# Second block of a two-block layer stack: projections with the weight tile stationary, so that they land transposed, and the forget bias added by VectorE

## What is computed

```python
h = x @ w_in                       # 2048 x (8*1536 + 12 + 4096)
qa, ka, va, za, qb, kb, vb, zb, f_logit, g_logit = split(h)
out_a = dilated_mixture(rope(qa), rope(ka), va)      # 12 heads of 128
log_f = log_sigmoid(f_logit + b_forget)              # 12 heads
out_b = softmax(qb kb^T * scale + D_t - D_s, causal) @ vb   # D = cumsum(log_f)
up_a = (out_a * silu(za)) @ w_up_a ; up_b = (out_b * silu(zb)) @ w_up_b
g_a, g_b = split(sigmoid(g_logit + b_gate))
y = (g_a * up_a + g_b * up_b) @ w_out
x = layer_norm(ALPHA * x + y, ln_g, ln_b)
```

## Time and profile before

| | |
|---|---|
| device time, median of 3 executions | 3028.01 us (3026.76 to 3030.45) |
| span of the profiled execution, first to last instruction | 3023.4 us |
| the profiled execution's own device time | not given apart from its span; the median is 4.6 us above the span |
| TensorE matmul busy | 2865.6 us (95%), 13536 matmuls |
| TensorE weight loads busy | 2356.3 us (78%) |
| VectorE busy | 1837.2 us (61%) |
| ScalarE busy | 1352.6 us (45%) |
| mean granted TensorE clock | 0.986 of 2.4 GHz |

### The profile page before, as it was taken

One profiled execution on the slowest core, in us unless ns is written; L12 is line 12 of the kernel. 1 busy time (PEld: TensorE's weight loads), 2 busy tenths in 40 slices (PEclk: granted clock), 3 DMA queues, 4 the chain that ended last, 5 costly groups with the idle time before them and its releaser, 6 DMA issues.

```text
span 3023.4 us, 38084 instructions
## 1 busy us (share of the span) xinstructions
PE 2865.6 (95%) x13536; PEld 2356.3 (78%) x13536; DVE 1837.2 (61%) x2035; ACT 1352.6 (45%) x1741; POOL 76.7 (3%) x88
## 2 busy tenths in 40 slices
PE   1699999899998999999999999979999999999997
PEld 1578887688887888888888888858888888788886
DVE  8888988677854655555444455565555544444565
ACT  1244554445543444444444444434445444444442
POOL 0400000000000000000000000010000000000000
PEclk9899999999999999999999999989999999999999
DMA  9887679576544555566554465635554654555663
GB/s 369 282 301 268 236 259 323 205 242 217 168 153 158 188 176 173 173 186 197 168 180 155 166 189 188 216 128 174 180 176 160 207 191 158 166 175 163 195 212 133
DMA packets 165005, 601.15 MB, mean 199 GB/s; under 512 B 19120, under 2 KB 19264, under 8 KB 163808
## 3 DMA queue, kind: packets, MB, share of 16 engines
q1 hardware_dynamic: 160336, 583.08, 57.3%
q0 software_dynamic: 4496, 15.74, 1.8%
HBM read 596.64 MB, written 2.10 MB: 198 GB/s over the span
## 4 chain that ended last, share of the span: by engine, by line
PE 66%; DVE 1%; issue 0%; ACT 0%; DMA 0%; DVEq 0%; ACTq 0%; SPq 0%
PE acc L724 60%; PE psT L648 1%; PE psS L673 1%; PE psS L688 1%; PE psS L677 1%; PE psT L654 1%; DVE x L597 0%; PE psS L695 0%; DVE wlo L414 0%; DVE x L601 0%; ACT whi L310 0%; DMA raw<-in_w 0%; DVE stage L446 0%; DVE x L572 0%; DVE stage L435 0%
## 5 line engine op out<-in xcount | busy, mean ns | idle before, releaser
L414 DVE TENSOR_TENSOR wlo<-raw,whi 128x1024 fp32r<-128x1024 f32 x672 | 822.7, 1225 | 905.1 <-ACT whi L310 902.0
L310 ACT ACTIVATE whi<-raw 128x1024 fp32r<-128x1024 f32 x672 | 711.8, 1060 | 1027.4 <-PE acc L724 1021.6
L724 PE MATMUL acc<-whi,xhi 128*128 128x512 f32 x2304 | 915.4, 397 | 8.4 <-DVE wlo L414 8.1
L724 PE MATMUL acc<-whi,xlo 128*128 128x512 f32 x2304 | 900.2, 391 | 0.0
L724 PE MATMUL acc<-wlo,xhi 128*128 128x512 f32 x2304 | 899.0, 390 | 0.0
L724 PEld LDWEIGHTS acc<-whi,xhi 128*128 128x128 f32 x2304 | 433.9, 188 | 100.2 <-DVE wlo L414 10.0
L724 PEld LDWEIGHTS acc<-whi,xlo 128*128 128x128 f32 x2304 | 433.4, 188 | 92.5
L724 PEld LDWEIGHTS acc<-wlo,xhi 128*128 128x128 f32 x2304 | 434.1, 188 | 85.8
L1240 ACT ACTIVATE whi<-raw 128x1024 fp32r<-128x1024 f32 x240 | 253.3, 1058 | 378.8 <-PE acc L1963 258.5
L1963 PE MATMUL acc<-whi,hhi 128*128 128x512 f32 x960 | 392.9, 409 | 16.2 <-DVE wlo L1425 6.7
L1425 DVE TENSOR_TENSOR wlo<-raw,whi 128x1024 fp32r<-128x1024 f32 x232 | 283.0, 1223 | 159.7 <-ACT whi L1240 158.7
(11 more groups left out here) (291 smaller groups left out, 2006.0 us busy)
## 6 DMA issues: line engine op xcount, KB each, us to landing
raw<-in_w SPq DMA_DIRECT2D x912, 512.0 KB, 3.4
mraw<-in_w_mod SPq DMA_DIRECT2D x150, 512.0 KB, 4.1
scr<-in_w_mod SPq DMA_DIRECT2D x31, 512.0 KB, 6.3
b_stage<-in_w_mod SPq DMA_DIRECT2D x11, 512.0 KB, 6.1
gate_row<-in_bg POOLq DMA_DIRECT2D x16, 256.0 KB, 4.5
x<-in_x SPq DMA_DIRECT2D x1, 2048.0 KB, 8.3
gain<-in_g_post POOLq DMA_DIRECT2D x2, 1024.0 KB, 6.5
gb<-in_ln_g POOLq DMA_DIRECT2D x2, 1024.0 KB, 5.0
```

Source lines behind the costliest of these rows:

```text
L310: act.activation(whi[:, n % SLOTS, :], raw[:, n % SLOTS, :], ACT.Copy).then_inc(s_hi, 1)
L414: dve.tensor_tensor(wlo[:, n % SLOTS, :], raw[:, n % SLOTS, :], whi[:, n % SLOTS, :].bitcast(F32), ALU.subtract).then_inc(s_lo, 1)
L724: m = pe.matmul(acc[c % 2][:, tb, :], a[:, kk, tile], b[:, n % SLOTS, k * CW:(k + 1) * CW], start=(kk == 0 and q == 0), stop=(kk == GK * g ...
```

## The change

q, k, z, g and u chunks ("turned") take the 128 x 128 tile of the weights as stationary operand and stream the 256 tokens: 24 matmuls of 256 columns per granule in place of 12 of 512. Their results have features on partitions, which is what the scores and the next products read, so the q, k, a and y transposes and their copies go. v goes first in a group, so that the order is v q k z; it and the o chunks keep the old form. The rotation works with tables that have features on partitions and writes `qT`, `kT`; its two halves become 64-partition operations. Gate bias is a per-partition value and goes into the sigmoid, which reads `acc`. The probabilities are divided before their transposes, and the product with v lands transposed too. For the forget bias GpSimd's queue writes `ncum` (12 x 256) to device memory and reads it back broadcast to 128 partitions into `gb`; VectorE adds the causal mask to its second half once, and adds bias and mask to the scores; the bias matmuls go. Positions r of the units move: scores from 23-25 to 27-29, p transposes from 28-30 to 33-35, o units from 33-34 to 38-39. The core of the diff (declarations, removed bodies and bookkeeping left out):

```diff
-            chunks += [(kind, 3 * half + grp) for kind in "qkvz"]
+            chunks += [(kind, 3 * half + grp) for kind in "vqkz"]
...
-        out += {12: [("q", grp, 0), ("q", grp, 1)], 20: [("k", grp, 0), ("k", grp, 1)], 28: [("p", grp, 0)],
-                29: [("p", grp, 1)], 30: [("p", grp, 2)], 38: [("a", grp, 0)], 39: [("a", grp, 1)]}.get(r, [])
...
+        out += {33: [("p", grp, 0)], 34: [("p", grp, 1)], 35: [("p", grp, 2)]}.get(r, [])
     return out
...
-        out += {23: [("s", grp, 0)], 24: [("s", grp, 1)], 25: [("s", grp, 2)],
-                33: [("o", grp, 0)], 34: [("o", grp, 1)]}.get(r, [])
+        out += {27: [("s", grp, 0)], 28: [("s", grp, 1)], 29: [("s", grp, 2)],
+                38: [("o", grp, 0)], 39: [("o", grp, 1)]}.get(r, [])
...
+def turned(kind):
+
+    return kind in "qkzgu"
...
-            for j in range(2 * NCW):
-                bias = dram["bg"][l * 2 * NCW + j].partition_broadcast(P)
...
-                pool.dma_start(gate_row[:, j % 2, :], bias).then_inc(s_grow[j % 2], 16)
+            if l:
+                pool.wait_ge(*acc_read(l - 1, CHUNKS2.index(("g", 2 * NCW - 1))))
+            pool.dma_start(bgT[:], dram["bg"][l]).then_inc(s_bias, 16)
+
+            pool.wait_ge(s_cum, l + 1)
+            pool.dma_start(dram["cum"], ncum[:]).then_inc(s_crow, 16)
+            pool.wait_ge(s_crow, at(l, 32, 16))
+            pool.dma_start(fbias, dram["cum"].partition_broadcast(P)).then_inc(s_crow, 16)
...
+            def part_hi(name):
+
+                h, _, k = dst_of(name)
+                act.activation(h[:, k:k + 2, :], part_src(name), ACT.Copy).then_inc(s_thi, 1)
...
+                if r == 11:
+                    evacuate(c0, v[:].rearrange("p b n -> p (b n)"), ACT.Copy)
+                if grp >= NR2 and r == 19:
+                    evacuate(c0 + 1, qT[:].rearrange("p h t -> p (h t)"), ACT.Copy, SCALE2)
+                if grp >= NR2 and r == 27:
+                    evacuate(c0 + 2, kT[:].rearrange("p h t -> p (h t)"), ACT.Copy)
...
+                if r == 35:
+                    evacuate(c0 + 3, zT[:].rearrange("p h t -> p (h t)"), ACT.Silu)
+                if r in (37, 38, 39):
+                    fill_copy(("p", grp, r - 37), probT[:, r - 37, :])
...
-                    if prev == "g" and g == 4:
...
-                        act.activation(t, t, ACT.Sigmoid).then_inc(s_gate, 1)
...
+                    if prev == "g" and g == 3:
...
+                        act.wait_ge(*multiplied(l, c - 1))
+                        for t in range(HPG):
+                            cols = slice(t * SEQ, (t + 1) * SEQ)
+                            last = act.activation(gates(j)[:, cols], accT[(c - 1) % 2][:, cols], ACT.Sigmoid,
+                                                  bias=bgT[:, HPG * j + t:HPG * j + t + 1])
+                        last.then_inc(s_acc[(c - 1) % 2], 1)
...
                 half = HD // 2
...
-                    link(last)
...
+                cos, sin = (tables[:, which, i, :].unsqueeze(1) for i in range(2))
+                dve.tensor_tensor(dst[:], src, cos.broadcast_to([P, HPG, SEQ]), ALU.mult)
+                dve.tensor_tensor(rtmp[0:half], src[half:P], sin[half:P].broadcast_to([half, HPG, SEQ]), ALU.mult)
+                dve.tensor_tensor(rtmp[half:P], src[0:half], sin[0:half].broadcast_to([half, HPG, SEQ]), ALU.mult)\
+                    .then_inc(s_acc[c % 2], 1)
+                dve.wait_ge(*acc_read(l, c))
+                dve.tensor_tensor(dst[:], dst[:], rtmp[:], ALU.add).then_inc(s_rope, 1)
...
+                if grp < NR2 and r == 19:
+                    rope(c0 + 1, 0, qT)
+                if grp < NR2 and r == 27:
+                    rope(c0 + 2, 1, kT)
+                if r in (31, 32, 33):
+
...
+                    if grp < NR2:
+                        m = (mask_a[:, 0:P] if u == 0 else mask_a[:, P:P + SEQ]).unsqueeze(1).broadcast_to([P, n, w])
+                    else:
+                        head = HPG * (grp - NR2) + max(0, 2 * (u - 1))
+                        m = fbias[:, head:head + n, 0:w]
+                        if (grp, u) == (NR2, 0):
+                            dve.wait_ge(s_cmask, l + 1)
...
                     p = prob[:, u, :].rearrange("p (h s) -> p h s", s=w)
-                    dve.tensor_tensor(p, psS[bank][:].rearrange("p (h s) -> p h s", s=w),
-                                      m.unsqueeze(1).broadcast_to([P, n, w]), ALU.add).then_inc(s_sfree[bank], 1)
+                    dve.tensor_tensor(p, psS[bank][:].rearrange("p (h s) -> p h s", s=w), m, ALU.add)\
+                        .then_inc(s_sfree[bank], 1)
...
+                    if grp >= NR2 and u == 0:
+                        link(dve.tensor_tensor(p, p, mask_b[:, 0:P].unsqueeze(1).broadcast_to([P, n, w]), ALU.add))
...
+                if r in (34, 35, 36):
+
+                    u = r - 34
+                    n, w, h0 = (HPG, P, 0) if u == 0 else (2, SEQ, 2 * (u - 1))
+                    dve.wait_ge(s_exp, at(l, 3 * NGRP, 3 * grp + u + 1))
+                    rows = rden[:, min(u, 1), h0:h0 + n]
+                    link(dve.reciprocal(rows, den[:, min(u, 1), h0:h0 + n]))
+                    p = prob[:, u, :].rearrange("p (h s) -> p h s", s=w)
+                    dve.tensor_tensor(p, p, rows.unsqueeze(2).broadcast_to([P, n, w]), ALU.mult).then_inc(s_pn, 1)
...
+                    t = zT[:, 2 * i:2 * i + 2, :]
+                    dve.tensor_tensor(t, psS[bank][:].rearrange("p (h t) -> p h t", t=SEQ), t, ALU.mult)\
                         .then_inc(s_sfree[bank], 1)
...
+                if r in (45, 46):
+                    part_lo(("a", grp, r - 45))
...
+                    if (c, g) == (F_CHUNK + 3, 1):
+
+                        dve.wait_ge(s_crow, at(l, 32, 32))
+                        late = fbias[:, :, P:SEQ]
+                        dve.tensor_tensor(late, late, mask_b[:, 2 * P:].unsqueeze(1).broadcast_to([P, NH2, P]),
+                                          ALU.add).then_inc(s_cmask, 1)
...
+                        for i in (1, 2):
+                            if grp < NR2:
+                                pe.wait_ge(s_rope, at(l, 2 * NR2, 2 * grp + i))
+                            else:
+                                pe.wait_ge(*acc_read(l, group_chunk(grp) + i))
...
-                        m = pe.matmul(out, qT[:, h, tb * P:(tb + 1) * P], kT[:, h, 0:w], start=True, stop=(grp < 3))
-                        if grp >= 3:
-
-                            head = HPG * (grp - 3) + h
-                            m = pe.matmul(out, ident[0:NH2, head:head + 1].broadcast_to([NH2, P]), ncum[:, 0:w],
-                                          start=False, stop=True)
+                        m = pe.matmul(out, qT[:, h, tb * P:(tb + 1) * P], kT[:, h, 0:w], start=True, stop=True)
...
+                    for h in (2 * i, 2 * i + 1):
+                        cols = slice(h * HD, (h + 1) * HD)
+                        for tb in range(TB):
+                            at_t = (h % 2) * SEQ + tb * P
+                            for s in range(tb + 1):
+                                u, col = (0, h) if tb == 0 else (1 + i, 2 * (h % 2) + s)
+                                m = pe.matmul(bank[:, at_t:at_t + P], v[:, s, cols], probT[:, u, col * P:(col + 1) * P],
+                                              start=(s == 0), stop=(s == tb))
...
-                        pe.wait_ge(*copied(l, ("y", g)))
+                        pe.wait_ge(*parted(l, ("y", g)))
...
+                    if turned(kind):
+                        steps = []
+                        for k in range(GK):
+                            kk = GK * g + k
+                            for t in range(HPG):
+                                col = k * CW + t * P
+                                for q, (b, a) in enumerate(((whi, ahead), (whi, alow), (wlo, ahead))):
+                                    m = pe.matmul(accT[c % 2][:, t * SEQ:(t + 1) * SEQ], b[:, n % SLOTS, col:col + P],
+                                                  a[:, kk, :], start=(kk == 0 and q == 0 and t % 2 == 0),
+                                                  stop=(kk == GK * granules2(c) - 1 and q == 2),
+                                                  skip_group_check=True)
```

More of the change, by code:

```diff
@@ L80, in group_step @@
     for q in range(len(CHUNKS2)):
-        if CHUNKS2[q][0] == "q" and q <= c:
+        if CHUNKS2[q][0] == "v" and q <= c:
             r = FIRST2[c] + g - FIRST2[q]
@@ L124 @@
 assert NF2 % 2 == 0 and NU2 % 2 == 0
-SPLIT2 = {name: i for i, name in enumerate([n for n in FILL2 if n[0] in "xay"])}
+PARTS2 = [("a", grp, i) for grp in range(NGRP) for i in range(HPG // 2)] + [("y", i) for i in range(KT // 2)]
+SPLIT2 = {name: i for i, name in enumerate([n for n in FILL2 if n[0] == "x"] + PARTS2)}
+NP2 = len(PARTS2)
+NR2 = 3
 NV2 = 2
-VLINKS2 = 47
+VLINKS2 = 50
+def turned(kind):
+    return kind in "qkzgu"
 def second_block(nc, ctx, x, rings, ps, dram, s_w, ident):
@@ L148, in second_block @@
```

(31 more changed lines are left out.)

165 lines of the change are left out of this document (57 added, 108 removed).

## The result

The change takes 3033.59 us (median of 15 executions, 3031.28 to 3037.13), the kernel before 3027.65 us beside it. The ratio is 1.0019, 95% interval 1.0012 to 1.0026: 6 us slower.

A forecast was written before the change was run, and what follows sets the result against it. TensorE's instruction list was taken to bound the kernel in the second block. The span 3023.4 - 39.0 - 34.3 + 7 + 2 = 2959.1 us, plus 4.6 carried over, gave 2964 us; range 2950 to 3012 us.

The forecast's parts named there:

- What bounds the kernel: Second block: time is the length of TensorE's list, so a microsecond off it is a microsecond off the end.
- What leaves the list: On TensorE: 352 transposes of stage, z and y go for 39.0 us, forget-bias products for 34.3 us; together 73.3 us.
- What the turned matmuls cost: 12288 matmuls of 256 columns on TensorE: load fits under the stream, step 0.1139 us, +7 us.
- The sum: Whole kernel: 3023.4 - 39.0 - 34.3 + 7 + 2 = 2959.1 us span, with 4.6 us added 2964 us.
- The 2 us for other engines: Allowance for tight places at the rotation of k and the division of probabilities, put at 0 to 6 us together.
- The 4.6: Microseconds by which the median of the kernel before lay above its profiled span, carried over to the forecast.
- Other engines: VectorE's rotation and division have 0.9 and 2 us to spare, GpSimd's broadcast costs 0; +2 us taken.
- the first, that the load comes out from under the stream: At each of 12288 turned matmuls the weight load shows; 3125 us at a 0.127 us step; 13% including full exposure.
- point of decision: Turned matmuls' step from which the exposed load decides: 0.1133 + 73.3/12288 = 0.1193 us.
- the full exposure: Every turned matmul pays its whole load: a pair takes 0.2229 us, kernel at some 4300 us; 1% of the 13%.
- Its sign: In the chain, 24 turned matmuls per granule taking 2.9 us or more would prove that the load comes out.
- The sign on the periods: Group periods of both halves equal, near 93 us (96.71 less 24 x 0.111 = 94.0, plus at most 0.8).

## Why the prediction was wrong

**What bounds the kernel**: right. The time went where TensorE's list went, in the change and in every experiment.

**What leaves the list**: right. The bias was put at 34.3 us and measured at 34.0 by itself. (The prediction counts 12 bias products in a group; there are 8, which take 16 of the matmul records, and the page's count fell by 96 in six groups, from 13536 to 13440. The price was read from the group's period and does not depend on it.) The transposes were put at 39.0 and never taken out alone. Turning alone cost 40.6 us; with 12288 x (0.1200 - 0.1133) = 82 us for the step, 41 or 42 are left for what it saves, which the transposes' 39 nearly cover.

**What the turned matmuls cost** is the step that failed. It said that the load "still fits under the stream, by 3.7 ns", took a step of 0.1139 us and gave 0.1151 as the near and 0.1175 as the far upper end. The step is 0.1200, outside the 0.113 to 0.115 that the prediction named as its own test: 82 us in place of 7. Each of the two bounds was nearly right by itself: the stream alone is 0.1134 in a steady run, the load alone 0.1116 (2 ns more than the short fp32 burst had shown). What was wrong is the longer of the two as the price of both. No row had a full load beside 256 fp32r columns, and the excess read from the fp32 scores, 1.8 ns, was for another kind of stream. The experiments show that at 128 and 256 columns some 7 ns come on top, and that in the long runs 16 fewer columns on either side end it, or nearly so.

**The sum** with the measured step: 3023.4 - 73.3 + 82 + 2 + 4.6 = 3038.7 us; the runs show 3033.6. The 2 us for other engines were not spent, and a group takes about 0.25 us less than its terms (96.71 - 24 x 0.111 + 576 x 0.0067 = 97.9), 3 us in twelve. The 4.6 was no fixed distance either: the profiled execution of the change took 3035.32 us with a span of 3033.6, 1.7 apart, so most of the 4.6 was the difference between one execution and the median. By part, q, k and z are 6912 matmuls, 46 us for 288 transposes or 32 us; g and u are 5376, 36 us for 64 transposes or 7 us. The periods agree: with turning alone each of the twelve groups takes 0.94 to 0.97 us more than before, some 11 us of the 40.6, and the rest, some 29, falls to g and u. So by this count no part of the turning pays, and g and u pay least; neither was run alone.

**Other engines**: right. The division and the rotation came in time, as TensorE has no wait for either, and the broadcast took 9.7 us where 12 were put.

**The rivals**: the first, that the load comes out from under the stream, happened in its mildest form. Its point of decision was a step of 0.1193 us, and the step is 0.1200. It had 13% with the full exposure, and its price was worked out for 0.127, far beyond that point. The range ended at 3012 us, for a step of 0.1175, so no step near the point of decision lay in it. Its sign was also set too far out: 24 turned matmuls take 2.88 us, short of the "2.9 us or more" that was to prove it, though 0.1193 makes 2.86. The sign on the periods was miscounted as well: "near 93 us" stands beside a sum of 94.0 to 94.8, and 97.65 was measured. The full exposure of the load did not happen: a pair takes 0.1200 us, not 0.2229. The 0.2229 is what the rule on row groups of the Trainium skill would have given ("TensorE: Matmul & The Clock Gate", Part 3, The mechanism); the runs disagree with it.

## What to carry to other kernels

When a change halves the columns of each matmul and doubles their number, look at the load behind each: where load and stream come within a few per cent of each other (0.1116 and 0.1134 us here), don't price the pair at the longer one, but allow for several per cent more (6% here), times every matmul. Work out the point of decision first; when the gain is spread over thousands of instructions a nanosecond of step is what decides, and the range must reach past that point. And take a change of two independent parts apart: here one was worth 34 us, and the other cost 41.

## What the runs showed that was not expected

- A load and a stream that is longer than it can still slow each other: 0.1116 us alone and 0.1134 us alone make 0.1200 together. In long runs the loss comes in over 112 to 128 loaded and 240 to 256 streamed columns.
- Between these ends the same instructions can keep either of two paces, 0.1136 or 0.118 us with 112 loaded columns. What in TensorE causes the loss, and what picks the pace, stays open; the order of the three matmuls does not matter in the change.
- Bias products of 12 rows among score products of 128 rows slow the score products as well, from 0.11 to 0.21 us a record.
- Fewer streamed columns do not shorten the stream by a fixed 0.443 ns each: with 64 loaded, 256, 224 and 192 columns take 0.1134, 0.1032 and 0.0887 us. This too is left without a cause.
